# HGRN2 trunk on one core: two levels of scores in one stage of TensorE, and a third pair of operand buffers

## What is computed

```python
q, fr, v, g = jnp.split(xn @ w_in, ...)
q = jax.nn.silu(q) * (HGRN_EXPAND ** -0.5)
f = lb + (1.0 - lb) * jax.nn.sigmoid(fr)
k = 1.0 - f
# S_t = diag(f_t) S_{t-1} + k_t v_t^T,  o_t = S_t^T q_t
A = jnp.einsum('bhtd,bhsd,bhtsd->bhts', qc, kc, jnp.exp(rel))   # rel = b_t - b_s, b = cumsum(log f), s <= t
o = jnp.einsum('bhts,bhsv->bhtv', A, vc) + ...
```

## Time and profile before

| | us |
|---|---|
| median of three runs | 2300.13 |
| lowest and highest run | 2299.28, 2300.26 |
| the profiled execution, its own time | 2299.77 |
| its span, from first to last instruction | 2297.9 |
| PE busy | 2285.5 (99%) |
| DVE busy | 1694.5 (74%) |
| ACT busy | 1049.6 (46%) |

### The profile page before, as it was taken

The page is one execution under the profiler, slowest core; times in us unless marked ns, Lnnn a source line. Parts: engine busy times, 40 slices in busy tenths (PEclk is TensorE's granted clock), DMA queues, the critical chain, the costliest instruction groups (busy, mean ns, idle before and its releaser), DMA issues.

```text
span 2297.9 us, 33410 instructions
## 1 busy us (share of the span) xinstructions
PE 2285.5 (99%) x11110; PEld 1916.0 (83%) x11110; DVE 1694.5 (74%) x2132; ACT 1049.6 (46%) x1089; POOL 2.8 (0%) x9
## 2 busy tenths in 40 slices
PE   9999999999999999999999999999999999999998
PEld 8888888888888888888888888888888888888887
DVE  7979788877878888865556676766878878876544
ACT  7444444454444454444444333444444444444443
POOL 0000000000000000000000000000000000000000
PEclk9999999999999999999999999999999999999999
DMA  7555555558888888875667888666888888887664
GB/s 247 166 174 160 179 164 166 183 189 236 242 245 233 244 243 240 242 214 188 191 191 208 243 238 245 202 193 197 248 242 240 242 244 236 241 249 219 220 192 155
DMA packets 389733, 493.55 MB, mean 215 GB/s; under 512 B 18704, under 2 KB 223888, under 8 KB 389520
## 3 DMA queue, kind: packets, MB, share of 16 engines
q1 hardware_dynamic: 388640, 490.01, 71.9%
q10 hardware_dynamic: 1008, 2.43, 0.3%
HBM read 459.85 MB, written 30.41 MB: 213 GB/s over the span
## 4 chain that ended last, share of the span: by engine, by line
PE 89%; DVE 6%; issue 3%; DMA 1%; ACT 1%; DVEq 0%; SPq 0%; ACTq 0%
PE acc L1459 24%; PE acc L1458 24%; PE acc L1460 24%; PE acc L1392 11%; PE acc L1402 6%; DVE w_parts L742 1%; DVE a_diag L1062 1%; DVE fpre L1047 1%; DMA raw<-in_hgrn_w_in 1%; DVE kl L1029 1%; PE side L1563 0%; DVE ql L1023 0%; ACT w_parts L463 0%; DVE ta L778 0%; DVE ta L769 0%
## 5 line engine op out<-in xcount | busy, mean ns | idle before, releaser
L742 DVE TENSOR_TENSOR w_parts<-raw,w_parts 128x1024 fp32r<-128x1024 f32 x816 | 992.8, 1224 | 551.8 <-ACT w_parts L463 425.6
L463 ACT ACTIVATE w_parts<-raw 128x1024 fp32r<-128x1024 f32 x815 | 860.1, 1059 | 1061.0 <-PE acc L1460 827.7
L1458 PE MATMUL acc<-w_parts,xn 128*128 128x512 f32 x1728 | 673.3, 390 | 0.0
L1460 PE MATMUL acc<-w_parts,xn 128*128 128x512 f32 x1728 | 672.6, 389 | 0.0
L1459 PE MATMUL acc<-w_parts,xn 128*128 128x512 f32 x1728 | 672.6, 389 | 0.0
L1458 PEld LDWEIGHTS acc<-w_parts,xn 128*128 128x128 f32 x1728 | 324.4, 188 | 67.5
L1460 PEld LDWEIGHTS acc<-w_parts,xn 128*128 128x128 f32 x1728 | 324.4, 188 | 67.2
L1459 PEld LDWEIGHTS acc<-w_parts,xn 128*128 128x128 f32 x1728 | 324.4, 188 | 66.9
L1458 PE MATMUL acc<-w_parts,act 128*128 128x512 f32 x704 | 274.3, 390 | 0.0
L1460 PE MATMUL acc<-w_parts,act 128*128 128x512 f32 x704 | 274.0, 389 | 0.0
L1459 PE MATMUL acc<-w_parts,act 128*128 128x512 f32 x704 | 274.0, 389 | 0.0
(11 more groups left out here) (157 smaller groups left out, 1223.0 us busy)
## 6 DMA issues: line engine op xcount, KB each, us to landing
raw<-in_ffn_w_up SPq DMA_DIRECT2D x352, 512.0 KB, 4.4
raw<-in_ffn_w_down SPq DMA_DIRECT2D x176, 512.0 KB, 4.6
raw<-in_hgrn_w_in SPq DMA_DIRECT2D x127, 512.0 KB, 3.8
raw<-in_sc_w_in SPq DMA_DIRECT2D x96, 512.0 KB, 4.6
crossing<-turned SPq DMA_DIRECT2D x54, 512.0 KB, 3.8
moved<-crossing SPq DMA_DIRECT2D x216, 128.0 KB, 4.5
raw<-in_hgrn_w_out SPq DMA_DIRECT2D x32, 512.0 KB, 4.0
raw<-in_sc_w_out SPq DMA_DIRECT2D x32, 512.0 KB, 4.7
```

Source lines behind the costliest of these rows:

```text
L463: nc.scalar.activation(w_parts[:, c % RING, :, 0, :], raw[:, c % RING], ACT.Copy).then_inc(hi_ready, 1)
L742: v.tensor_tensor(w_parts[:, c % RING, :, 1, :], raw[:, c % RING], w_parts[:, c % RING, :, 0, :].bitcast(F32), ALU.subtract).then_inc(lo_r ...
L1458: mm(bank, x_hi, hi, start=begin and q == 0, stop=False)
L1460: high = mm(bank, x_lo, hi, start=False, stop=end and q == KC - 1)
```

## The change

Levels 1 and 2, 3 and 4, 5 and 6 share a stage each: the first level of a pair goes into columns 0 to 511 of the buffer and the second into 512 to 1023, and both are multiplied where the second one was (behind steps 6, 10 and 13). DVE takes the two one behind the other in the step after, with a `link` and a raise of `stage_seen` between them, so levels 1, 3 and 5 are taken one, two and one step later than before. Since level 4's operands are formed before level 3's are used, there is a third pair of operand buffers, in the tile `pad`, which is idle in this phase; `OPERANDS_IN` says which level uses which. The operands are formed in the same steps as before (`OPERANDS_AT`). PAIRS becomes two stages of 256 columns behind the same step 3, each with a take of its own, so that a pass has eight stages where it had ten and their number stays even. The exception of step 13 is gone. The diff, without blank lines:

```diff
-LEVEL, OUTPUT = range(2)
-PLAN = [(3, LEVEL, 0), (5, LEVEL, 1), (6, LEVEL, 2), (8, LEVEL, 3), (10, LEVEL, 4),
-        (12, LEVEL, 5), (13, LEVEL, 6), (14, LEVEL, -1), (15, LEVEL, 7), (17, OUTPUT, 0)]
-LEAD = 2
-TAKE_FIRST_AT = 13
+PAIRS, LEVEL, OWN, FULL, OUTPUT = range(5)
+PLAN = [(3, PAIRS, 0), (3, PAIRS, 1), (6, LEVEL, 1), (10, LEVEL, 3), (13, LEVEL, 5), (14, OWN, 0), (15, FULL, 7),
+        (17, OUTPUT, 0)]
+OPERANDS_AT = {1: 3, 2: 4, 3: 6, 4: 8, 5: 10, 6: 11, 7: 13}
+OPERANDS_IN = [0, 1, 0, 2, 1, 0, 2, 1]
 FOLD_AT = 3
 FOLD_OUT_AT = 4
 HGRN_STAGES = len(PLAN)
...
+        queries = [ql[:, 0], ql[:, 1], pad[:, :, TAPS - 1:TAPS - 1 + P]]
+        keyed = [kl[:, 0], kl[:, 1], pad[:, :, TAPS - 1 + P:]]
...
                 pre, su = halves(fpre[:], n), halves(suf[:], n)
-                buf = m % 2
-                q_to = ql[:, buf].rearrange("p j (w n) -> p (j w) n", n=n)
+                q_to, k_to = queries[OPERANDS_IN[m]], keyed[OPERANDS_IN[m]]
+                q_spans = q_to.rearrange("p j (w n) -> p j w n", n=n)
+                q_from, pre_from = (t[:].rearrange("p j (w z n) -> p j w z n", z=2, n=n)[:, :, :, 1] for t in (qh, fpre))
                 if n == 1:
-                    link(v.tensor_tensor(q_to, halves(qh[:], n)[:, :, 1], pre[:, :, 1], ALU.mult), i)
-                    v.tensor_tensor(kl[:, buf].rearrange("p j (w n) -> p (j w) n", n=n), q_to, halves(kh[:], n)[:, :, 0],
-                                    ALU.mult).then_inc(product_ready, 1)
+                    link(v.tensor_tensor(q_spans, q_from, pre_from, ALU.mult), i)
+                    v.tensor_tensor(k_to.rearrange("p j (w n) -> p (j w) n", n=n), q_to.rearrange("p j (w n) -> p (j w) n", n=n),
+                                    halves(kh[:], n)[:, :, 0], ALU.mult).then_inc(product_ready, 1)
                     v.memset(su[:, :, 1], 1.0)
                     mark(v.tensor_copy(su[:, :, 0], pre[:, :, 1]))
                     return
-                v.tensor_tensor(q_to, halves(qh[:], n)[:, :, 1], pre[:, :, 1], ALU.mult)
+                v.tensor_tensor(q_spans, q_from, pre_from, ALU.mult)
                 if n == P:
-                    v.tensor_tensor(kl[:, buf], kh[:, :, 0:P], suf[:, :, 0:P], ALU.mult).then_inc(qk_ready, 1)
+                    v.tensor_tensor(k_to, kh[:, :, 0:P], suf[:, :, 0:P], ALU.mult).then_inc(qk_ready, 1)
                     return
-                k_to = kl[:, buf].rearrange("p j (w z n) -> p j w z n", z=2, n=n)
+                k_spans = k_to.rearrange("p j (w z n) -> p j w z n", z=2, n=n)
                 for b in range(T // P):
-                    o = v.tensor_tensor(k_to[:, :, :, b], keys(kh, b, n), keys(suf, b, n), ALU.mult)
+                    o = v.tensor_tensor(k_spans[:, :, :, b], keys(kh, b, n), keys(suf, b, n), ALU.mult)
                 o.then_inc(qk_ready, 1)
                 dve.wait_ge(qk_ready, at(i, len(LEVELS), m + 1))
                 shape = [P, TG * T // (2 * n), n]
...
+            def take_level(m, src, heads=slice(0, TG)):
+                n, at_mask, count = LEVELS[m], T + m * P, heads.stop - heads.start
+                mask = masks[:, at_mask:at_mask + P].rearrange("p (w n) -> p w n", n=n)
+                return v.copy_predicated(
+                    a_diag[:, heads].rearrange("p j b (w z n) -> p j (b w) z n", z=2, n=n)[:, :, :, 1],
+                    mask[:, None].to_broadcast([P, count, P // n, n]),
+                    src.rearrange("p (j w n) -> p j w n", j=count, n=n))
             def take_stage(i, stage):
                 s = S_HGRN + stage
-                _, _, m = PLAN[stage]
+                _, what, m = PLAN[stage]
                 src = side[:, s % STAGES]
-                if m < 0:
+                if what == OWN:
                     mask = masks[:, None, 0:T].to_broadcast([P, TG, T])
                     o = v.copy_predicated(a_diag[:].rearrange("p j b t -> p j (b t)"), mask,
                                           src.rearrange("p (j t) -> p j t", j=TG))
-                elif LEVELS[m] < P:
-                    n = LEVELS[m]
-                    at_mask = T + m * P
-                    mask = masks[:, at_mask:at_mask + P].rearrange("p (w n) -> p w n", n=n)
-                    o = v.copy_predicated(
-                        a_diag[:].rearrange("p j b (w z n) -> p j (b w) z n", z=2, n=n)[:, :, :, 1],
-                        mask[:, None].to_broadcast([P, TG, P // n, n]),
-                        src[:, 0:TG * P].rearrange("p (j w n) -> p j w n", j=TG, n=n))
+                elif what == PAIRS:
+                    o = take_level(0, src[:, 0:GC // 2], slice(m * TW, (m + 1) * TW))
+                elif what == LEVEL:
+                    link(take_level(m, src[:, 0:GC]), i)
+                    v.sem_inc(stage_seen, 1)
+                    o = take_level(m + 1, src[:, GC:2 * GC])
                 else:
                     o = v.tensor_copy(a_off[:], src[:, 0:TG * P].rearrange("p (j t) -> p j t", j=TG))
                 o.then_inc(stage_free, 1)
...
-                    if what == LEVEL and g * HGRN_IN.cpg + kk - 2 * HGRN_IN.cpg == after + 2:
+                    if what != OUTPUT and g * HGRN_IN.cpg + kk - 2 * HGRN_IN.cpg == after + 2:
...
                     product_low_parts(i, 1, tb[:], own_parts)
-                done = [stage for stage, (after, what, _) in enumerate(PLAN) if what == LEVEL and n == after + 1]
+                done = [stage for stage, (after, what, _) in enumerate(PLAN) if what != OUTPUT and n == after + 1]
                 for stage in done:
                     dve.wait_ge(stage_done, at(i, HGRN_STAGES, S_HGRN + stage + 1))
                     v.sem_inc(stage_seen, 1)
-                for after, what, m in PLAN:
-                    if what == LEVEL and 0 <= m < len(LEVELS) - 1 and n == (after - LEAD + 1 if m else 1):
+                if n == 1:
+                    prefixes(i, 0)
+                for m, begin in OPERANDS_AT.items():
+                    if n == begin + 1 and m < len(LEVELS) - 1:
                         prefixes(i, m)
-                if n == TAKE_FIRST_AT:
-                    for stage in done:
-                        take_stage(i, stage)
-                for after, what, m in PLAN:
-                    if what == LEVEL and m > 0 and n == after - LEAD:
+                for m, begin in OPERANDS_AT.items():
+                    if n == begin:
                         level_operands(i, m)
-                if n != TAKE_FIRST_AT:
-                    for stage in done:
-                        take_stage(i, stage)
+                for stage in done:
+                    take_stage(i, stage)
             phase_of(HGRN_IN, hgrn, ahead=levels, into=lambda g: ta)
             late[0] += 4 * HGRN_IN.n
...
-                column = n % TG * P
-                mm(side[:, n // TG % STAGES, column:column + P], ones[:], ones[:], start=True, stop=True)
+                column = n % (2 * TG) * P
+                mm(side[:, n // (2 * TG) % STAGES, column:column + P], ones[:], ones[:], start=True, stop=True)
...
-            def level_steps(m):
+            def level_steps(m, column=0):
+                q, k = queries[OPERANDS_IN[m]], keyed[OPERANDS_IN[m]]
                 if LEVELS[m] == P:
-                    return [lambda to, j=j: mm(to[:, j * P:(j + 1) * P], kl[:, m % 2, j], ql[:, m % 2, j], start=True,
-                                               stop=True) for j in range(TG)]
-                return [lambda to, j=j, r=r: mm(near(to[r * HALF:(r + 1) * HALF, j * P:(j + 1) * P], m, r),
-                                                kl[:, m % 2, j, r * HALF:(r + 1) * HALF], near(ql[:, m % 2, j], m, r),
+                    return [lambda to, j=j: mm(to[:, j * P:(j + 1) * P], k[:, j], q[:, j], start=True, stop=True)
+                            for j in range(TG)]
+                return [lambda to, j=j, r=r: mm(near(to[r * HALF:(r + 1) * HALF, column + j * P:column + (j + 1) * P], m, r),
+                                                k[:, j, r * HALF:(r + 1) * HALF], near(q[:, j], m, r),
                                                 start=True, stop=True) for j in range(TG) for r in range(2)]
             def hgrn(i, first, g, kk):
...
                         continue
-                    if what == LEVEL:
-                        if m < 1:
-                            parts, halves = (own_parts, 2) if m < 0 else (pair_parts, 1)
-                            pe.wait_ge(product_parts_ready, at(i, 2, 1 - m))
-                            steps = [lambda to, c=c, n=n: mm(to[:, c * GC:(c + 1) * GC], sum_ones[:],
-                                                             parts[:, n, c * GC:(c + 1) * GC], start=(n == 0),
-                                                             stop=(n == 1))
-                                     for c in range(halves) for n in range(2)]
-                        else:
-                            pe.wait_ge(qk_ready, at(i, len(LEVELS), m + 1))
-                            steps = level_steps(m)
```

(16 more changed lines are left out.)

## The result

The changed kernel takes 2307.23 us, median of seven runs (2305.22 to 2308.35), against 2299.28 for the kernel before, seven runs beside it on the same chip (2298.81 to 2300.26). The ratio is 1.0034, 95% interval 1.0022 to 1.0045. It is slower by 7.9 us, outside my range of 2300.0 to 2306.7, and slower by over 0.2%, which I had given 0.33.

A forecast was written before the change was run, and what follows sets the result against it. DVE was taken to set each pass's end, with PE waiting at FULL for level 6's take. Four passes at 1.11 us, 4.4 in all, on 2299.77 gave 2304.2 us (chance 0.55), range 2300.0 to 2306.7.

The forecast's parts named there:

- What bounds the kernel: Last 47 us of each pass: DVE sets the end, PE keeps it company, so saved PE time returns as a wait.
- DVE's sum: DVE work added ahead of level 6's take: 0.06 for PAIRS plus 1.05 for three links, 1.11 us a pass.
- the row of the transposes: Trace gap from transposes L874 to the split, semaphore raised behind a wait: 0.23 us, taken for each of three links.
- 0.04: Small gap, L1017 to L1018, where the next instruction itself carries the wait; as a rival 2302.0 us, chance 0.20.
- PAIRS in halves: DVE's take of PAIRS as two instructions of 256 elements instead of one of 512: 0.06 us more.
- The padded tile: DVE's operand writes into `pad` were claimed to cost no more than those into `kl`: nothing added.
- The free links: Rival: linked DVE takes follow as close as unlinked ones, leaving 0.06 us a pass; 2300.0 us, chance 0.06.
- the rule behind them: Skill page on DVE: the next operation waits for an empty pipeline, so a semaphore after each costs nothing extra.
- PE's side: Each merged pair of level stages saves PE one opening, taken as 0.25 us, so 0.75 for three a pass.
- A wait of 2.4 us in place of one of 0.52: PE stands ready for FULL at 205.39, but level 6's take ends at 207.72; the earlier wait was before OWN.
- The register gap: Rival: DVE computing wait values in a register adds 0.19 us per link in loop passes; 2306.0 us, chance 0.13.
- OUTPUT's copy: Copy into `a_off`, awaited by the next pass's output stage, was said to move with FULL; no cost of its own.

## Why the prediction was wrong

- **What bounds the kernel: right.** DVE sets the end of each pass, PE's saved time came back as a wait, and that wait moved from OWN to FULL in all four passes.
- **DVE's sum, 1.11 a pass: 0.92, too high by a fifth.** The gap of a link is not 0.23, the row of the transposes, nor 0.04, but 0.15, in all twelve places together 2.2 us with one of 0.5:

```profile
DVE a_diag L1057 <- DVE a_diag L1057: 2.2, 12, 0.5
...
107.97 0.72 DVE L1057 COPY_PREDICATED a_diag<-masks,side 128x512 f32<-128x512 uint8 x1 [0.51 <-DVE a_diag L1057]
...
186.39 0.73 DVE L1057 COPY_PREDICATED a_diag<-masks,side 128x512 f32<-128x512 uint8 x1 [0.15 <-DVE a_diag L1057]
```

  From the first take of a pair to the second are 1.45 (184.94 to 186.39), 0.86 and 0.87 us, where an unlinked neighbour begins after 1.11, 0.61 and 0.61: 0.34 + 0.25 + 0.26 = 0.85. Another 0.1 lies between the end of the last take and FULL's matmuls (the 0.14 of the chain above, for the 0.05 of the earlier trace rows). PAIRS in halves, put at 0.06, cost nothing: its two takes show 1.31 together and the next instruction begins 1.10 after the first, as behind the single take of level 0 before (174.48 to 175.58). The padded tile cost nothing, as said.
- **The free links, and the rule behind them: refuted.** Each link cost 0.25 to 0.34 us. The trace disagrees with the Trainium skill, page "VectorE: DVE Perf Modes", section "The DRAIN you can't avoid", by which a semaphore after each operation costs nothing extra. The links here do more than raise one, since the next take also waits for it. The same section says that a next operation that is not held starts earlier, which fits the unlinked takes, so the disagreement is over the price of a link alone.
- **PE's side, 0.75 a pass: 0.94,** by the two kernels in which PE alone sets the pace. It had no weight in the sum, since DVE gated.
- **The step that failed** is "A wait of 2.4 us in place of one of 0.52", and what I made of it: nothing. I had the wait right (2.2 in three passes, 2.8 in pass 0) and priced it as time in which PE merely stands. But PE comes out of it at half its clock in some passes, 1.6 us each, two in the profiled run: 3.2 of the 7.1 us. Without them the time would have been 2299.77 + 1.12 + 2.76 = 2303.7, inside the range. Behind the waits of PE in the trace of before, 1.3 us at most, the clock did not fall; it held none of 2.4 from which to read the price. The one place of that trace with the lower clock is not among the rows. It is the end of the program, behind PE's last matmul:

```profile
2290.00:2294.00 4.00, 0.38 (x2) 0.00 (x0) 2.16 (x5) 2.26 (x5) 0.00 (x0) 1.00 0.63 230
2294.00:2297.90 3.90, 0.00 (x0) 0.00 (x0) 0.00 (x0) 0.00 (x0) 0.00 (x0) 0.57 0.71 257
```

  From 2290.4 PE has nothing to do, and somewhere behind 2294 the clock is at half. A wait of 2.4 lies between 1.3, behind which nothing fell, and these 3.6 us and more: a fall was to be kept as an unknown cost with both ends, nothing and half the rate for some microseconds in four passes, and the range would have reached past 2307.
- **The register gap, my slower rival (2306.0): wrong mechanism.** Its time came near by chance. The loop's passes show 0.15 in all nine of their links. The one longer gap, 0.51, stands in pass 0, which is unrolled; its cause stays open.
- **What follows the gate: too short-sighted.** I wrote that OUTPUT's copy moves with FULL, and for this change it does. But between FULL's buffer, FULL's operands and OUTPUT's copy lie gaps of under 2 us, and the kernels with takes in steps 13 and 12 only walked from one to the next. The bound was DVE's whole list up to the next thing that PE needs, not one take. With the copy moved forward DVE does as much as before (1696.0 us busy, 1696.4 in the change) and no longer holds PE.

What stays open is what decides in which pass the clock falls: equal waits of 2.5 us gave two of four, and the runs of the changed kernel spread over 3.1 us (2305.22 to 2308.35). Of the eleven changed kernels whose profile shows no fall nine spread over 0.9 to 1.5 us, but levels 5 and 6 apart over 2.3 and OWN twice over 2.8, so a wide spread is no sure sign of falls. How many falls each execution without a profile had is not known.

## What to carry to other kernels

Merging work on the engine that waits is worth nothing until the engine that gates has room: list every join behind the one that is removed, and move them all before a gain is promised (here the merges alone cost 7.9 us and the copy alone gained nothing, while merges, early takes and early copy together won 6.0). A new wait of TensorE is to be priced by its length twice: as time, and from about 2 us on, by these runs, as a possible fall of the clock behind it. Where a wait cannot be avoided, even useless products that shorten it can pay.

## What the runs showed of the hardware

- The granted clock fell behind a wait of 2.0 to 2.8 us in 9 of 16 passes (four profiles, with and without merges), behind 3.4 to 3.7 us in 4 of 4, and behind 1.3 to 1.9 us in none of 12 profiled passes (repeated OWN, released buffer, take repeated twice). A fall behind the shorter waits cost 1.5 to 1.6 us, behind the longest up to 2.9.
- A linked take on DVE begins 0.15 us after the end of the take ahead where a semaphore is raised behind the wait (once 0.51, in pass 0 of the change, and there again in the five kernels that keep its takes of levels 5 and 6 in step 14); unlinked instructions begin 0.10 to 0.20 before that end. Putting other work between the takes gained only 0.2 us a pass, since gaps of 0.13 and 0.23 then stand behind the second takes.
- The take of level 0 in two instructions of 256 elements costs DVE as much as in one of 512: the next instruction begins 1.10 us after its start either way.
